# An MLP's second product by Strassen's scheme, over pairs of token tiles, in a four-layer decoder trunk on eight cores

## The chip, the cores and the metric

The kernel runs on the 8 NeuronCores of one Trainium2 chip. Each core takes one of the 8 sequences of the batch and works alone on it, with all weights. The time is device time in microseconds of the slowest core. A measurement of this kernel is the median of some runs; the three runs of the kernel before lie between 3194.84 and 3195.68 us.

## What is computed

The input is (8, 2048, 1024) in float32. Four layers follow each other, then a last RMSNorm. Each layer adds a token mixer and then an MLP to the residual x:

```python
for i in range(4):
    h = rmsnorm(x, norm_mix[i])
    x = x + mixer[i % 3](h)          # A: chunked gMLP, B: pooling, C: Conformer convolution
    h = rmsnorm(x, norm_mlp[i])
    x = x + jnp.square(jax.nn.relu(h @ m_w1[i])) @ m_w2[i]   # 1024 -> 4096 -> 1024
out = rmsnorm(x, norm_final)
```

So the layers' mixers are A, B, C, A. An MLP is two products, each of 2048 x 1024 x 4096 per core.

## The kernel before

**Layout.** x stays in SBUF in float32 for the whole kernel, transposed (`xT`: 128 partitions, 8 chunks `kc` of the width, 2048 tokens), as four token tiles `tt` of 512. Products are in bf16: a matmul takes a 128x128 block of weights as the stationary operand and 512 tokens as the moving one, and accumulates in one of 8 PSUM banks (128 x 512 float32). Weights come by DMAs that GpSimd issues, into a ring of five slots of 8 KB per partition (`take_slot`, `load_w`); the DMA turns float32 into bf16.

**Order.** The kernel is first written down as a list of operations (`sc.op`) with an estimated cost each; `Sched.schedule` (L219) then makes, in advance, an order for each engine: among the operations that can start earliest it takes the one written first. It also gives out the banks, and holds two back for older operations (`RESERVE`). The order on each engine is fixed from then on; semaphores keep the dependencies. Every operation is issued from a helper, so all rows of the profile show its line, L161, and are told apart by the tiles that they write and read.

**MLP** (`mlp`, L678). The inner width of 4096 is cut into 8 blocks `fb` of 512. `W1(fb, tt)` makes 4 groups of 8 matmuls into a bank each; VectorE applies the ReLU and the norm's factor `rst` (one `scalar_tensor_tensor` from the bank to a float32 buffer `rl`), ScalarE squares it into the bf16 tile `aT`. `W2(fbs, tt)` makes 8 groups, one for each output chunk `dc`, of 4 matmuls per `fb`; after each group VectorE adds the bank to x (`add_to_x`, L665). W1 of the next pair (fb, tt) is written ahead of W2 of the current one. The outer loop goes over `fb`, the inner over the four tiles, so each weight block is loaded once. In layers 0, 2 and 3 the last two blocks share their bank in W2. Ahead of the first use of a tile, `prep` scales x by the norm's gain into h (half the chunks on ScalarE, half on VectorE) and sums the squares (squares on ScalarE, sums on GpSimd or VectorE, one matmul to sum over partitions, then logarithm and exponential on ScalarE).

**Passes.** When a tile has had its last block, `after_tile` of the next mixer starts that mixer's norm of the tile: A for tile 0, B for tiles 0 and 1 and the factors of the others, C scaled copies `c_h` of all four tiles and their sums of squares, with a spill of part of x to HBM. Mixer C's first product needs all four tiles, since it takes every sixteenth token. Mixer A's gate tables `a_S` (`setup`, L788: 24 small VectorE operations, two loads by SyncE, a mask on GpSimd) are made within the MLP ahead of it, in layer 0 within its own body (L1016). In the last layer the last tile's W2 is cut into 256, 128 and 128 columns, so that the final norm and the store can start early. The folded weights of mixer B are made at the head of its body (L1098), before its first product S1(0).

Of the kernel before, what the change touches and what calls it, by code (L numbers as in the profile page):

```python
# [15 lines left out]
KC = 8  # L16
# [65 lines left out]

class Res:
# [41 lines left out]
    def split(self, n):  # L125

        l = []
        for _ in range(n):
            x = Res()
            x.w, x.r = set(self.w), set(self.r)  # L130
            l.append(x)
        self.subs += l
        return l
# [30 lines left out]
def MM(out, lhsT, rhs, start, stop):  # L164
    return I("matmul", out, lhsT=lhsT, rhs=rhs, start=start, stop=stop)

# [253 lines left out]
def c_dve(n=512, mode=1):  # L420
    return 0.09 + n / (960.0 * mode)
# [10 lines left out]
HT_OFF = 54 * KB  # L432
# [3 lines left out]
def build_program(S, layers, final):  # L436
# [32 lines left out]
    if layers:  # L469
        din("m_w1", (4, 8, 128, 4096))  # L470
        din("m_w2", (4, 8, 128, 4096))
# [36 lines left out]
    epst, (eps_res,) = pers("epst", (128, 1), F32)  # L508
    mhalf, (mh_res,) = pers("mhalf", (128, 4), F32)
# [64 lines left out]
    sc.op("dve", I("memset", epst[:], EPS), wr=[eps_res])  # L574
    sc.op("pool", I("memset", mhalf[:], -0.5), wr=[mh_res])
# [8 lines left out]
    def sum_squares(tt, acc, acc_r, eng="pool", after=(), cs=slice(0, 512)):  # L584

        n = cs.stop - cs.start
        for kc in range(KC):
            sq, sq_r = (sacc, sacc_r) if kc == 0 else next_sq()[::2]
            sc.op("act", I("activation", out=sq[:, cs], in_=xs(kc, tt)[:, cs], func=AF.Square),
                  rd=[xr(kc, tt, cs)], wr=[sq_r], cost=c_act(n), after=after, tag="sq")  # L590
            if kc:
                last = kc == KC - 1
                sc.op(eng, I("tensor_tensor", out=acc[:, cs] if last else sacc[:, cs], in0=sacc[:, cs], in1=sq[:, cs], op=ALU.add),
                      rd=[sq_r, sacc_r] if last else [sq_r], wr=[acc_r if last else sacc_r],
# [63 lines left out]
    def rmsnorm(tt, gcol, hT, hr, mode="pool", rs=None, after=()):  # L658
        rs, rs_r = rs or rms(tt, None, mode, after=after)
        for kc in range(KC):  # L660
            sc.op("dve", I("scalar_tensor_tensor", out=hT[:, kc, :], in0=xs(kc, tt),
                           scalar=pv[:, gcol + kc:gcol + kc + 1], in1=rs, op0=ALU.mult, op1=ALU.mult),
                  rd=[xr(kc, tt), rs_r, pv_res], wr=[hr[kc]], cost=c_dve(), port=True, tag="hT")

# [4 lines left out]
    def mix_h(i):  # L669
# [4 lines left out]
    PLACES = {0: ((0, 8, 16, 30), (24, 26, 28, 38), (70, 74, 40), (78, 80, 82)),  # L674
              1: ((54, 0, 8, 32), (50, 40, 42, 44), (46, 66), (52, 62, 64)),
              2: ((0, 8, 16, 24), (46, 48, 50, 52), (32, 36, 62), (40, 42, 44))}

    def mlp(l, after_tile, mode, last, setup):  # L678
        gcol = PCOLS[f"norm_mlp{l}"]
        p_h, p_rs, p_a, p_rl = PLACES[l % 3]  # L680
        hT, aT, rl, rst, w = [], [], [], [], {}

        def prep(tt):
            hT.append(zone(f"mh{tt}", (128, KC, 512), BF16, p_h[tt] * KB, KC))
            h, hr = hT[tt]
            rst.append(zone(f"mrs{tt}", (128, 512), F32, p_rs[tt] * KB))
            for kc in range(KC):
                scale_x(kc, tt, gcol, h[:, kc, :], [hr[kc]], "dve" if kc % 2 else "act")
            rms(tt, (rst[tt][0][:], rst[tt][1][0]), mode[tt])

        def load(fb):
            w[fb] = (load_w("m_w1", l, fb, (8, 512)),
                     load_w("m_w2", l, fb, (4, 1024)))

        def W1(fb, tt):
            if fb == 0:
                prep(tt)
# [25 lines left out]
        def W2(fbs, tt, parts=((0, 512),)):  # L723

            for p0, p1 in parts:
# [10 lines left out]
                while ends:  # L736
                    ends.pop()()
# [888 lines left out]
```

How the kernel before makes its waits and increments, by code:

```python
            def body(e):  # L382
                table = None
                if eng == "act":
                    table = "lnexp"
                    e.preload_act_table_set(TABLES[table])
                for lst, o in plan[eng]:
                    for k, v in lst:
                        e.wait_ge(sems[k], v)
                    if o.table is not None and o.table != table:
                        table = o.table
                        e.preload_act_table_set(TABLES[table])
                    for f in o.fns[:-1]:
                        f(e)
                    o.fns[-1](e).then_inc(sems[o.pos], 1 if o.dma is None else 16)
                if eng == "sp":
                    for k in self.dma_keys:
                        if per.get(k) and known["sp"].get("D_" + k, 0) < 16 * len(per[k]):
                            e.wait_ge(sems["D_" + k], 16 * len(per[k]))
                    for f in self.ENGS:
                        if f != "sp" and known["sp"].get("E_" + f, 0) < cnt["E_" + f]:
                            e.wait_ge(sems["E_" + f], cnt["E_" + f])
```

## Time and profile before

| | |
|---|---|
| median of three runs | 3195.46 us |
| profiled execution, slowest core (5), span | 3193.6 us |
| spans of the eight cores | 3186.4 to 3193.6 us |
| TensorE busy, matmuls | 3163.5 us (99%), 16042 |
| VectorE, ScalarE, GpSimd busy | 1988.0, 976.4, 510.4 us |
| mean granted TensorE clock | 0.997 to 0.998 |

The profile records one execution of its own; its time is known as the spans of its cores, and the runs of the first row are others of the same program. Busy times are sums over the instructions of an engine, shares are of the span. A matmul's duration (379 ns for 512 columns) overlaps the next one's; the interval between starts is what counts. "Idle before, releaser" is how long the engine stood still ahead of a group and what ended that.

### The profile page before, as it was taken

What the parts mean: (1) busy time and instruction counts of PE and PEld (TensorE: products, weight loads), DVE (VectorE), ACT (ScalarE), POOL (GpSimd) and SP (SyncE); (2) the same over time, 40 slices, a digit from 0 to 9 for tenths busy, and PEclk for the clock granted to TensorE, in tenths of its full rate; (3) what the DMA queues carried; (4) which work ended last, traced back from release to release, by engine and by line L of the source; (5) the groups of instructions that cost most, each with busy time, mean ns of one, the idle gap of its engine ahead of it and who ended that gap; (6) DMA issues with size and microseconds to landing.
All of it is one profiled execution on the core that took longest, in us unless ns stands there. A gap on an engine that the chain in (4) does not pass through costs nothing.

```text
span 3193.6 us, 45998 instructions; the slowest of 8 cores (3186.4 to 3193.6 us)
## 1 busy us (share of the span) xinstructions
PE 3163.5 (99%) x16042; PEld 1518.9 (48%) x16042; DVE 1988.0 (62%) x3152; ACT 976.4 (31%) x1621; POOL 510.4 (16%) x527
## 2 busy tenths in 40 slices
PE   8999999999999999999999999999999999999999
PEld 4444444444444444444576444444444444444444
DVE  8945665665556965665558666654755757466556
ACT  4312433211134431112634511121322333311124
POOL 1111322100022010000551300010212141200011
PEclk9999999999999999999999999999999999999999
DMA  9599898122216412221422422214898987522202
GB/s 169 105 158 169 158 163 136 27 40 40 40 25 109 72 27 40 40 39 20 109 46 81 67 53 41 40 27 68 138 162 131 155 147 136 92 40 38 42 14 106
DMA packets 82398, 264.44 MB, mean 83 GB/s; under 512 B 4992, under 2 KB 8192, under 8 KB 82176
## 3 DMA queue, kind: packets, MB, share of 16 engines
q0 software_dynamic: 64992, 231.49, 43.3%
q1 hardware_dynamic: 17184, 30.02, 3.0%
q8 instruction: 135, 2.21, 0.3%
q14 instruction: 87, 0.71, 0.1%
HBM read 479.34 MB, written 13.63 MB: 154 GB/s over the span
## 4 chain that ended last, share of the span: by engine, by line
PE 97%; DMA 1%; ACT 1%; DVE 1%; issue 0%; POOL 0%; SPq 0%; DVEq 0%; ACTq 0%; POOLq 0%
PE bank L161 97%; DMA xT<-x 1%; DMA ring_46<-b_w_out 0%; DMA ring_45<-a_w_in 0%; DVE sacc L161 0%; ACT ring_47 L161 0%; DVE xT L161 0%; SPq L161 0%; DVE c_y L161 0%; ACT c_h_138 L161 0%; ACT L392 0%; ACT hraw_75 L161 0%; DVE c_z_166 L161 0%; POOL sacc L161 0%; ACT xT L161 0%
## 5 line engine op out<-in xcount | busy, mean ns | idle before, releaser
L161 DVE TENSOR_TENSOR xT<-bank,xT 128x512 f32<-128x512 f32 (+2 forms) x1040 | 707.6, 683 | 449.8 <-PE bank L161 439.4
L161 ACT ACTIVATE a_uT<-bank,pv 128x512 bf16<-128x512 f32 x96 | 65.6, 686 | 145.1 <-PE bank L161 141.8
L161 ACT ACTIVATE a_uTv_192<-bank,pv 128x512 bf16<-128x512 f32 x96 | 65.9, 686 | 96.4 <-PE bank L161 96.3
L161 ACT ACTIVATE a_vv_188<-bank 128x512 bf16<-128x512 f32 x96 | 56.9, 597 | 102.4 <-DVE bank L161 102.3
L161 DVE SCALAR_TENSOR_TENSOR bank<-bank,pv,a_Sv_182 128x512 f32<-128x512 f32 x96 | 71.5, 757 | 25.7 <-PE bank L161 25.6
L161 DVE SCALAR_TENSOR_TENSOR bank<-bank,pv,a_S 128x512 f32<-128x512 f32 x96 | 71.2, 755 | 25.2 <-PE bank L161 25.0
L161 POOL TENSOR_TENSOR sacc<-sacc,sq_58 128x512 f32<-128x512 f32 (+1 forms) x52 | 65.0, 1250 | 108.8 <-ACT sq_58 L161 58.4
L161 DVE BATCH_NORM_STATS2 a_stv_190<-a_vv_188 128x6 f32<-128x512 bf16 x96 | 65.7, 687 | 26.6 <-ACT a_vv_188 L161 26.6
L161 POOL TENSOR_TENSOR sacc<-sacc,sq_56 128x512 f32<-128x512 f32 (+1 forms) x52 | 65.1, 1253 | 102.2 <-ACT sq_56 L161 93.4
L161 DVE TENSOR_TENSOR bank<-bank,a_bvbv_189 128x512 f32<-128x512 f32 x96 | 66.1, 688 | 17.7 <-PE bank L161 17.7
L161 DVE TENSOR_TENSOR a_uTv_192<-bank,a_uTv_192 128x512 bf16<-128x512 f32 x96 | 65.1, 689 | 11.7 <-DVE bank L161 9.5
L161 POOL TENSOR_TENSOR sacc<-sacc,sq_60 128x512 f32<-128x512 f32 (+1 forms) x52 | 65.7, 1264 | 36.3 <-ACT sq_60 L161 26.7
L161 DVE TENSOR_TENSOR a_uT<-bank,a_uT 128x512 bf16<-128x512 f32 x96 | 64.9, 687 | 9.6 <-DVE bank L161 8.7
L161 ACT ACTIVATE sq_58<-xT 128x512 f32<-128x512 f32 (+1 forms) x84 | 52.0, 619 | 53.7 <-POOL sacc L161 26.8
L161 ACT ACTIVATE sq_56<-xT 128x512 f32<-128x512 f32 (+1 forms) x84 | 51.8, 616 | 46.3 <-DVE xT L161 24.9
L161 ACT ACTIVATE sq_60<-xT 128x512 f32<-128x512 f32 (+1 forms) x84 | 52.0, 619 | 42.0 <-DVE xT L161 23.1
L392 ACT ACT_TABLE_LOAD x19 | 24.4, 1283 | 130.1 <-DVE bank L161 111.3
L161 ACT ACTIVATE a_v<-bank 128x512 bf16<-128x512 f32 x72 | 42.4, 596 | 68.5 <-DVE bank L161 68.3
L161 DVE BATCH_NORM_STATS2 a_st<-a_v 128x6 f32<-128x512 bf16 x72 | 48.9, 687 | 16.9 <-ACT a_v L161 16.8
L161 POOL DMA_DIRECT2D ring_45<-m_w x14 | 10.0, 716 | 274.6 <-PE bank L161 274.6
L161 POOL DMA_DIRECT2D ring_48<-m_w x13 | 9.4, 719 | 250.7 <-PE bank L161 231.6
L161 POOL DMA_DIRECT2D ring_47<-m_w x12 | 8.6, 717 | 253.2 <-PE bank L161 253.2
(924 smaller groups left out, 6680.9 us busy)
## 6 DMA issues: line engine op xcount, KB each, us to landing
ring_46<-a_w_in POOLq DMA_DIRECT2D x19, 1024.0 KB, 12.0
ring_45<-a_w_in POOLq DMA_DIRECT2D x19, 1024.0 KB, 11.9
ring_44<-a_w_in POOLq DMA_DIRECT2D x18, 1024.0 KB, 13.4
ring_48<-a_w_in POOLq DMA_DIRECT2D x17, 1024.0 KB, 12.8
ring_47<-a_w_in POOLq DMA_DIRECT2D x15, 1024.0 KB, 13.4
ring_45<-m_w POOLq DMA_DIRECT2D x14, 1024.0 KB, 8.7
ring_48<-m_w POOLq DMA_DIRECT2D x13, 1024.0 KB, 8.9
ring_44<-m_w POOLq DMA_DIRECT2D x13, 1024.0 KB, 8.3
```

Of the source, the lines that this page charges most:

```text
L161: return lambda e: getattr(e, _method)(*[_r(a) for a in args], **{k: _r(v) for k, v in kwargs.items()})
L392: e.preload_act_table_set(TABLES[table])
```

## The change

The second product of the MLP is computed by Strassen's scheme in Winograd's form. The outer loop takes pairs of token tiles (`p`), the inner one four blocks `b` of 1024 of the inner width. For a pair and a block, the activations are A11, A12 (first tile, both halves of the block) and A21, A22 (second tile), the weights W11 to W22 (first digit: half of the block, second digit: output chunk d or d + 4). `G1` makes the activations with the first product; its ReLU runs on ScalarE within the bank where h already carries the norm's factor, and on VectorE for tiles 0 and 1 of layer 2. `sums` makes four sums of activations, `load2` loads four weight tiles of one d and makes four sums of them, all in bf16 on VectorE. `G2` makes seven products of four matmuls each into four banks; two banks are accumulated into after they have been read, and each read of a bank is an add into x (eight per d). The very last block of the last layer stays plain (`plain_block`, with the cuts of before). Since p is the outer loop, `m_w1` and `m_w2` are loaded once per pair, hence twice; a load of `m_w2` is half as large as before. h of tiles 0 and 1 is made during the mixer before (`early`), that of tiles 2 and 3 in steps between the G2 of the first pair; the next mixer's norms of tiles 0 and 1 in steps during the second pair. Mixer A's `setup` is always in its body, mixer B's comes after S1(0), and the places of the buffers are new. The diff, cut to its core:

```diff
+def MORE(out, lhsT, rhs, start, stop):
+    return I("matmul", out, lhsT=lhsT, rhs=rhs, start=start, stop=stop, skip_group_check=True)
...
-    return 0.09 + n / (960.0 * mode)
+    return 0.155 + n / (960.0 * mode)
...
+    H_BLK = 4
+    POOL_OFF = 32 * KB
+    POOL_N = 53
+    def c_fast(n=512):
+        return 0.09 + n / 1900.0
...
+        def prep(tt, mode):
+            if raw_first and tt < 2:
+                h[tt] = mix_h4(tt)
+                hT, hr = h[tt]
+                for kc in range(KC):
+                    scale_x(kc, tt, gcol, hT[:, kc, :], [hr[kc]], "dve" if kc % 2 else "act")
+                rst[tt] = rms(tt, None, mode)
+                yield
+            else:
+                if tt == 2:
+                    rsx_.append(zone("m_rsx", (128, 512), F32, POOL_OFF + POOL_N * KB))
+                rs = rms(tt, (rsx_[0][0][:], rsx_[0][1][0]) if tt >= 2 else None, mode)
+                yield
+                h[tt] = mix_hall(tt) if l % 3 == 1 else mix_h4(tt)
+                yield from rmsnorm_steps(tt, gcol, *h[tt], rs=rs)
...
+        def G1(p, b, i):
+            if i % 2 == 0:
+                w1[(p, b, i // 2)] = load_w("m_w1", l, b * 2 + i // 2, (32, 128))
+            w, wr_ = w1[(p, b, i // 2)]
+            for n, t in ((0, 1), (1, 1), (0, 0), (1, 0)):
+                tt = 2 * p + t
+                hT, hr = h[tt]
                 bk = Bank()
+                for k0, k1 in ((0, 6), (6, 7), (7, 8)) if raw_first and first[0] else ((0, KC),):
+                    sc.op("pe", [MM(bk.v(), w[:, (i % 2 * 2 + n) * KC + kc, :], hT[:, kc, :], kc == 0, kc == KC - 1)
+                                 for kc in range(k0, k1)], rd=[wr_] + hr[k0:k1], wr=[bk], cost=c_pe(k1 - k0), tag="W1")
+                if tt in rst:
+                    sc.op("dve", I("scalar_tensor_tensor", out=bk.v(), in0=bk.v(), scalar=0.0, in1=rst[tt][0],
+                                   op0=ALU.max, op1=ALU.mult), rd=[rst[tt][1]], wr=[bk], cost=c_dve(), tag="relu")
+                else:
+                    sc.op("act", I("activation", out=bk.v(), in_=bk.v(), func=AF.Relu), wr=[bk], cost=c_act(), tag="relu")
+                a, ar = A[(p, b, i, "A%d%d" % (t + 1, n + 1))] = tile()
+                sc.op("act", I("activation", out=a[:], in_=bk.v(), func=AF.Square), rd=[bk], wr=[ar], cost=c_act(), tag="sqr")
+            first[0] = False
+        def comb(out, o_r, x, x_r, y, y_r, op):
+            sc.op("dve", I("tensor_tensor", out=out, in0=x, in1=y, op=op), rd=[r for r in (x_r, y_r) if r is not o_r], wr=[o_r],
+                  cost=c_fast(), port=True, tag="comb")
+        def sums(p, b, i):
+            def get(k):
+                return A[(p, b, i, k)]
+            def put(k, x, y, op, to=None):
+                t, r = A[(p, b, i, k)] = to or tile()
+                comb(t[:], r, get(x)[0][:], get(x)[1], get(y)[0][:], get(y)[1], op)
+            put("S1", "A21", "A22", ALU.subtract)
+            put("m2", "A11", "S1", ALU.subtract)
+            put("m3", "A21", "A11", ALU.subtract, get("A21"))
+            put("n4", "A12", "m2", ALU.subtract)
+        def load2(b, d, plain=False):
+            t, r, key = take_slot()
+            last_load[0] = sc.op("pool", I("dma_start", out=t[:, 0:2048], in_=dram["m_w2"][l, b * 4 + d], max_dma_last_dim=8192), wr=[r],
+                                 cost=0.95, dma=key, nbytes=512 * 2048, tag="load")
+            w_ops.append(last_load[0])
+            v = {k: t[:, j * 512:(j + 1) * 512] for j, k in enumerate(("W11", "W12", "W21", "W22", "T1", "n2", "T4"))}
+            vr = dict(zip(v, r.split(7)))
+            if not plain:
+                comb(v["T1"], vr["T1"], v["W12"], vr["W12"], v["W11"], vr["W11"], ALU.subtract)
+                comb(v["W12"], vr["W12"], v["W22"], vr["W22"], v["W12"], vr["W12"], ALU.add)
+                comb(v["n2"], vr["n2"], v["W22"], vr["W22"], v["T1"], vr["T1"], ALU.add)
+                comb(v["T4"], vr["T4"], v["W21"], vr["W21"], v["n2"], vr["n2"], ALU.subtract)
+            return {k: v[k].rearrange("p (i c) -> p i c", i=4) for k in v}, vr
+        def G2(p, b, d):
+            w, wr_ = load2(b, d)
+            x11, x12, x21, x22 = ((d, 2 * p), (d + 4, 2 * p), (d, 2 * p + 1), (d + 4, 2 * p + 1))
+            a, f, e, g = Bank(), Bank(), Bank(), Bank()
+            def prod(bk, ak, wk, start, outs):
+                mm = MM if start else MORE
+                ts = [A[(p, b, i, ak)] for i in range(H_BLK)]
+                sc.op("pe", [mm(bk.v(), w[wk][:, i, :], ts[i][0][:], start and i == 0, i == H_BLK - 1) for i in range(H_BLK)],
+                      rd=[wr_[wk]] + [r for _, r in ts], wr=[bk], cost=c_pe(4), tag="W2")
+                for dc, tt in outs:
+                    add_to_x(dc, tt, bk)
+            prod(a, "A11", "W11", True, [x11])
+            prod(f, "A12", "W21", True, [x11])
+            prod(e, "m3", "W12", True, [x22])
+            prod(a, "m2", "n2", False, [x21])
+            prod(g, "n4", "W22", True, [x12])
+            prod(e, "A22", "T4", False, [x21])
+            prod(a, "S1", "T1", False, [x12, x22])
...
+        early = [prep(tt, "pool") for tt in range(2)]
+        yield early
+        for e in early:
+            run_all(e)
+        pipe = [(p, b) for p in range(2) for b in range(4)]
+        for i in range(H_BLK):
+            G1(0, 0, i)
+            sums(0, 0, i)
+        for j, (p, b) in enumerate(pipe):
+            more = j + 1 < len(pipe)
+            if (p, b) == (0, 0):
+                work.extend(prep(tt, "pool") for tt in (2, 3))
+            if (p, b) == (1, 0):
+                work.extend(gen_store(tt) if last else nxt.after_steps(tt) for tt in (0, 1))
+            if (p, b) == (1, 3) and not last:
+                work.extend(iter(nxt.late_steps(tt)) for tt in (0, 1))
+            while (p, b) == (0, 3) and work:
+                step()
+            for i in range(H_BLK):
+                plain = last and not more
+                if more and i < H_BLK - 1:
+                    G1(*pipe[j + 1], i)
+                if not plain:
+                    G2(p, b, i)
+                elif i == 0:
+                    while work:
+                        step()
+                    plain_block(p, b)
+                if more:
+                    if i == H_BLK - 1:
+                        G1(*pipe[j + 1], i)
+                    if not (last and j + 2 == len(pipe)):
+                        sums(*pipe[j + 1], i)
+                step()
+        while work:
+            step()
+        if not last and nxt:
+            for tt in (2, 3):
+                run_all(nxt.after_steps(tt))
+                run_all(nxt.late_steps(tt))
...
+    hall = nc.alloc_sbuf_tensor_at("hall", [128, KC, S], BF16, offset=Z0)
+    def mix_hall(tt):
+        return hall[:, :, tt * 512:(tt + 1) * 512], [Res(Z0 + kc * 2 * S + tt * 1024, Z0 + kc * 2 * S + tt * 1024 + 1024) for kc in range(KC)]
...
-                    if first:
-                        self.setup(UOFF, after=third[:1])
+                    self.setup(UOFF, after=third[:1])
...
+        def after_steps(self, tt):
+            h, hr = mix_hall(tt)
+            for j, kc in enumerate(KORDER):
+                self.hr[kc][tt] = hr[kc]
+                scale_x(kc, tt, self.gcol, h[:, kc, :], [hr[kc]], "act")
+                if tt < 2 and j % 2:
+                    yield
+            sp_dma(f"spill{tt}", x_spill[tt], xT[:, 3:8, tt * 512:(tt + 1) * 512], rd=[xr(kc, tt) for kc in range(3, 8)],
+                   nbytes=128 * 5 * 2048)
+            yield
+        def late_steps(self, tt):
             if not self.started:
                 self.start()
-            h = self.h
-            xg = [scale_x(kc, tt, self.gcol, h[kc][:, tt * 512:(tt + 1) * 512], [self.hr[kc][tt]], "act") for kc in range(KC)]
-            if tt < NT - 1:
-                sum_squares(tt, self.acc[:, tt * 512:(tt + 1) * 512], self.acc_r[tt])
-            else:
-                sum_squares(tt, self.acc[:, tt * 512:(tt + 1) * 512], self.acc_r[tt], "dve", after=[xg[5]])
-            sp_dma(f"spill{tt}", x_spill[tt], xT[:, 3:8, tt * 512:(tt + 1) * 512], rd=[xr(kc, tt) for kc in range(3, 8)],
-                   nbytes=128 * 5 * 2048)
-        def body(self, first):
+            sum_squares(tt, self.acc[:, tt * 512:(tt + 1) * 512], self.acc_r[tt], "dve" if tt == NT - 1 else "pool", order=KORDER,
+                        run=(rsb[0][0], rsb[0][1][0]) if tt == NT - 1 else None)
...
-        shared["m_w1"] = tiles(f("m_w1"), 8, 512)
-        shared["m_w2"] = tiles(f("m_w2"), 4, 1024)
+        w1 = f("m_w1").reshape(-1, KC, 128, 4, 2, 2, 2, 128).transpose(0, 3, 5, 2, 6, 4, 1, 7)
+        shared["m_w1"] = w1.reshape(-1, 8, 128, 4096)
+        w2 = f("m_w2").reshape(-1, 4, 2, 4, 128, 2, 4, 128).transpose(0, 1, 6, 4, 2, 5, 3, 7)
+        shared["m_w2"] = w2.reshape(-1, 16, 128, 2048)
```

## Rows read from the trace of the kernel before

**Rows 1.** Cores: span and mean granted TensorE clock (core 5 is on the second die).
```profile
core 0: 3186.4 us, clock 0.998
...
core 5: 3193.6 us, clock 0.997
```
**Rows 2.** The page's busy line: us, share of the span, instructions of each engine.
```profile
PE 3163.5 (99%) x16042; PEld 1518.9 (48%) x16042; DVE 1988.0 (62%) x3152; ACT 976.4 (31%) x1621; POOL 510.4 (16%) x527
```
**Rows 3.** Chain of waits: shares of the span by engine.
```profile
PE 97%; DMA 1%; ACT 1%; DVE 1%; issue 0%; POOL 0%; SPq 0%; DVEq 0%; ACTq 0%; POOLq 0%
```
**Rows 4.** Windows: us, busy us (instructions) by engine, granted clock, DMA share, GB/s.
```profile
80.00:160.00 80.00, 80.00 (x443) 39.16 (x441) 74.82 (x139) 26.29 (x41) 10.84 (x18) 1.00 0.60 106
...
544.00:986.00 442.00, 441.99 (x2048) 200.24 (x2047) 258.98 (x378) 119.44 (x196) 57.42 (x56) 1.00 0.23 41
...
592.70:648.00 55.30, 55.30 (x258) 25.09 (x257) 33.25 (x49) 10.07 (x16) 1.43 (x2) 1.00 0.21 39
```
**Rows 5.** Timeline of TensorE, two W2 calls: start us, us, operation.
```profile
1540.35 7.07 PE L161 MATMUL bank<-aT0v_130,ring_45 128*128 128x512 bf16 x32
1547.25 7.07 PE L161 MATMUL bank<-aT1v_133,ring_45 128*128 128x512 bf16 x32
```
**Rows 6.** Waits of TensorE from 60 to 3160 us: sum us, times, longest.
```profile
PE bank L161 <- DMA ring_46<-b_w_out: 2.2, 1, 2.2
...
PE bank L161 <- ACT c_h_139 L161: 1.3, 1, 1.3
```
**Rows 7.** Groups of VectorE by form: busy us, mean ns, idle before.
```profile
L161 DVE TENSOR_TENSOR xT<-bank,xT 128x512 f32<-128x512 f32 x1016 | 700.8, 691 | 447.3 <-PE bank L161 436.9 <-issue 0.3
...
L161 DVE BATCH_NORM_STATS2 a_stv_190<-a_vv_188 128x6 f32<-128x512 bf16 x96 | 65.7, 687 | 26.6 <-ACT a_vv_188 L161 26.6
...
L161 DVE TENSOR_TENSOR sacc<-sacc,sq_60 128x512 f32<-128x512 f32 x20 | 13.7, 687 | 5.3 <-ACT sacc L161 3.3 <-ACT sq_60 L161 1.1 <-DVE sacc L161 0.9
...
L161 DVE SCALAR_TENSOR_TENSOR rl_89<-bank,mrs_92 128x512 f32<-128x512 f32 x11 | 7.6, 692 | 10.5 <-PE bank L161 10.5
...
L161 DVE SCALAR_TENSOR_TENSOR a_S<-bank,pv,a_bs 128x128 f32<-128x128 f32 x24 | 6.4, 343 | 0.0
...
L161 DVE SCALAR_TENSOR_TENSOR hT_73<-xT,pv,rs_64 128x512 bf16<-128x512 f32 x8 | 5.5, 745 | 1.6 <-ACT rs_64 L161 1.6
...
L161 DVE TENSOR_TENSOR xT<-bank,xT 128x128 f32<-128x128 f32 x16 | 3.9, 284 | 1.6 <-PE bank L161 1.6
...
L161 DVE TENSOR_SCALAR hT_74<-xT,pv 128x512 bf16<-128x512 f32 x8 | 3.6, 491 | 6.5 <-DMA xT<-x 6.5
...
L161 DVE TENSOR_TENSOR xT<-bank,xT 128x256 f32<-128x256 f32 x8 | 3.0, 417 | 0.9 <-PE bank L161 0.9
...
L161 DVE TENSOR_TENSOR c_T_156<-ring_47,c_mask 128x1536 bf16<-128x1536 bf16 x1 | 0.9, 948 | 0.0
```
**Rows 8.** Groups of ScalarE by form.
```profile
L161 ACT ACTIVATE a_vv_188<-bank 128x512 bf16<-128x512 f32 x96 | 56.9, 597 | 102.4 <-DVE bank L161 102.3
...
L161 ACT ACTIVATE mh_85<-xT,pv 128x512 bf16<-128x512 f32 x4 | 2.7, 709 | 0.0
```
**Rows 9.** Timeline of VectorE within a W2 call.
```profile
2962.71 0.69 DVE L161 TENSOR_TENSOR xT<-bank,xT 128x512 f32<-128x512 f32 x1 [0.17 <-PE bank L161]
2963.57 0.69 DVE L161 TENSOR_TENSOR xT<-bank,xT 128x512 f32<-128x512 f32 x1 [0.17 <-PE bank L161]
```
**Rows 10.** Tile mh3v_180 (ns min/median/max, first and last start), and GpSimd's adds.
```profile
L161 DVE TENSOR_SCALAR mh3v_180<-xT,pv x4: 474/981/1490, 1768.5 to 1781.5; 128x512 bf16<-128x512 f32 x4
...
L161 POOL TENSOR_TENSOR sacc<-sacc,sq_60 128x512 f32<-128x512 f32 x50 | 63.5, 1270 | 35.9 <-ACT sq_60 L161 26.7 <-POOL sacc L161 4.5 <-ACT sacc L161 3.2
```
**Rows 11.** DMA: the whole span, one queue in 592.7 to 648, an issue row.
```profile
DMA packets 82398, 264.44 MB, mean 83 GB/s; under 512 B 4992, under 2 KB 8192, under 8 KB 82176
...
q0 software_dynamic: 542, 2.09, 20.7%
...
ring_44<-m_w POOLq DMA_DIRECT2D x13, 1024.0 KB, 8.3
```

More of the change, by code:

```diff
@@ L431 @@
 KB = 1024
-HT_OFF = 54 * KB
+HT_OFF = 0
 SM_OFF = 70 * KB
@@ L582, in next_sq, with sum_squares @@
         return sqb[sqn[0] % NSQ]
[L584 removed]
+    def sum_squares(tt, acc, acc_r, eng="pool", after=(), cs=slice(0, 512), order=range(KC), run=None):
         n = cs.stop - cs.start
[L587 to L588 removed]
+        run, run_r = run or (sacc, sacc_r)
+        for k, kc in enumerate(order):
+            sq, sq_r = (run, run_r) if k == 0 else next_sq()[::2]
             sc.op("act", I("activation", out=sq[:, cs], in_=xs(kc, tt)[:, cs], func=AF.Square),
                   rd=[xr(kc, tt, cs)], wr=[sq_r], cost=c_act(n), after=after, tag="sq")
[L591 to L594, printed above, removed]
+            if k:
+                last = k == KC - 1
+                sc.op(eng, I("tensor_tensor", out=acc[:, cs] if last else run[:, cs], in0=run[:, cs], in1=sq[:, cs], op=ALU.add),
+                      rd=[sq_r, run_r] if last else [sq_r], wr=[acc_r if last else run_r],
                       cost=c_pool(n) if eng == "pool" else c_dve(n), port=True, tag="sqadd")
@@ L663, in rmsnorm, with run_all @@
                   rd=[xr(kc, tt), rs_r, pv_res], wr=[hr[kc]], cost=c_dve(), port=True, tag="hT")
+            if k % 2:
+                yield
+    def run_all(steps):
+        for _ in steps or ():
+            pass
+    def rmsnorm(*args, **kwargs):
+        run_all(rmsnorm_steps(*args, **kwargs))
     def add_to_x(dc, tt, bk, cs=slice(0, 512)):
@@ new lines, in plain_block, with step, gen_store @@
+            ends.pop()()
+        ends = []
+        work = []
+        def step(n=1):
+            for _ in range(n):
+                if work and next(work[0], work) is work:
+                    work.pop(0)
+        def gen_store(tt):
+            end = nxt(tt)
+            yield
+            end()
+        early = [prep(tt, "pool") for tt in range(2)]
[6 more added lines that the diff above has]
+            sums(0, 0, i)
@@ L1030, in body @@
                     self.norm(tt + 1, after=[late_u[0]])
+                else:
+                    for e in early:
+                        run_all(e)
                 WO(tt, mid)
@@ L1182, in body @@
                         self.norm(tt + 2)
+                if tt in (1, 2):
+                    next(early[tt - 1])
+                elif tt == 3:
+                    for e in early:
+                        run_all(e)
                 S2(tt)
```

233 lines of the change are left out of this document (97 added, 136 removed).

## The prediction

> **What bounds the kernel now.** I first looked at the cores: all eight lie within 7.2 us, and the granted clock is 0.998 in core 0 and 0.997 in core 5, that is the 2.4 GHz level on either die [rows 1]. The profile is of core 5, span 3193.6 us. The median of the runs is 3195.46 us, so about 1.9 us lie around the span; I make the sum against the span and add them. Next the page's busy line [rows 2]: TensorE 99%, VectorE 62%, ScalarE 31%. The chain of waits says the same, 97% of it matmuls [rows 3]. The windows show that the MLP stages are the purest case [rows 4]: in 544 to 986 (layer 0's MLP) 2048 matmuls fill 442.0 us without a gap, 0.2158 us each; the timeline gives 32 matmuls from 1540.35 to 1547.25, 6.90 us, 0.2156 each [rows 5]. The list of what TensorE waited for has no entry from an MLP stage except the end of the last one; between 60 and 3160 us it holds nine entries that sum to 9.8 us, none over 2.2, of which some 2.6 us are the pass from layer 1's MLP to mixer C and 2.2 us a late `b_w_out` load [rows 6]. So time here is the number of matmuls, as long as the other engines keep up.
>
> **What the change takes away.** A block is one pair of token tiles by 1024 of the inner width. The second product of a block is now 2 tiles x 8 output chunks x 8 = 128 matmuls; with seven products for eight it is 4 values of d x 7 products x 4 = 112. There are 4 layers x 2 pairs x 4 blocks = 32 blocks, of which the very last stays plain: 31 x 16 = 496 matmuls fewer. They sit in stages where TensorE never rests, so each is worth its full interval: 496 x 0.216 = **107.1 us**. The first product keeps its count, and so do the norms. All matmuls stay 128x128 by 512 in bf16.
>
> **VectorE.** (a) Per block 16 sums of activations and 16 of weights, all 128x512 in bf16 from SBUF to SBUF, 992 in all. No row has this shape. From above: an fp32 sum of 512 takes 687 to 691 ns; from below: the bf16 product of 1536 elements takes 948 ns [rows 7]. The adds of 512, 256 and 128 columns (691, 417, 284) give a fixed 150 ns or so [rows 7]; (948 - 150)/1536 = 0.52 ns per element, so 150 + 266 = 416 ns. I take 0.416 us, since the 948 row has the same operation, type and memory, and keep 0.69 as the upper end, 0.32 (948/3) as the lower. (b) The adds into x: a block needs 4 x 8 = 32. Before, a layer needed 224 (six blocks of 512 one by one, two merged), layer 1 had 256. Now 256 each, and 232 wide ones in the last layer for 216: 80 more of 0.691, 55 us. (c) The ReLU leaves VectorE except for tiles 0 and 1 of layer 2: 512 - 64 = 448 fewer of 0.691, minus 310 us. (d) Preparing h: eight 0.745 ops for fourteen tiles, against four cheaper scalings, about +50 us. Sum: 413 + 55 - 310 + 50 = +208 us, 1988 to 2196, or 71% of the new span. In an ordinary block: 32 x 0.691 + 32 x 0.416 = 35.4 us in 240 x 0.216 = 51.8 us of matmuls, 68%; now it is 33.3 in 55.3, 60% [rows 4]. In the first half of layer 2 each step (32 + 28 matmuls, 12.96 us) also has 4 ReLUs and a share of the preparation of tiles 2 and 3: 5.53 + 3.33 + 2.76 + 0.75 = 12.4 us, 95%. The window 80 to 160 has VectorE at 74.8 of 80 us, 94%, with TensorE at 80.0 [rows 4]: such a load alone stops nothing. I put 3 us on these 16 steps for what the order written out in advance gets wrong, with 0 and 30 as ends.
>
> **ScalarE and the banks.** The 448 ReLUs go there, PSUM to PSUM. The nearest row is PSUM to SBUF, 597 ns, and a scaled copy within SBUF takes 709 [rows 8]; I take 0.6, with 0.71 as the upper end (21.0 us a block, still 40%). With squares of about 0.6 too: 19.2 of 51.8 us, 37%, and 976 + 448 x 0.6 - 14 x 4 x 0.71 = 1205 us in the whole. That hides beside TensorE. But a bank is now held for ReLU and square, some 1.3 us with the semaphores, instead of 0.7. A group of eight matmuls takes 1.73 us, so the first product holds two to three banks, and the second product four. Seven of eight: it fits.
>
> **The new wait.** Bank a gets three products and bank e two; each next one must wait until the adds have read the last. Two other products (8 matmuls, 1.73 us) lie between. From the timeline of adds [rows 9]: one starts every 0.86 us, takes 0.69 and leaves 0.17 idle. A matmul is 0.379 long at an interval of 0.216, so a result is there some 0.2 us after its product's turn; add 0.69 and the semaphore, and the bank is free 0.95 to 1.0 us after the product, 0.7 before it is wanted. One sum (0.42) pushed in between doesn't use that up, two would. Behind a waiting product stand all later matmuls of TensorE's queue, the next G1 as well; the planner orders them by its own costs (0.36 for a sum, where I have 0.416). Its planned order is kept, so I charge 3 us for 124 G2 calls, with ends 0 and 0.3 us each (37 us).
>
> **GpSimd.** What the profile shows of VectorE beside it: a scaling of 512 elements has 491 ns for tile 0's `hT_74`, but 474, 981 and 1490 for `mh3v_180`, while GpSimd's adds of 1270 ns run [rows 7, 10]. The Trainium skill (SBUF — State Buffer, "Who interferes with whom") says that a VectorE instruction with two SBUF inputs and a GpSimd instruction that reads SBUF block each other for a whole instruction. By it every bf16 sum beside such an add could wait up to 1.27 us; the trace agrees in kind by the 981. In the rows alone: a layer's MLP has 28 such adds, at most 36 us of VectorE in some 415, which lifts it from about 72% to 81%, below the 94% seen with a full TensorE. I charge nothing in the ordinary blocks; in layer 2 it is within the end of 30 above.
>
> **Loads.** Both weights are now read once per pair, so the 64 loads of 1024 KB become twice as many bytes, 67.1 MB more, 331.5 in all [rows 11]. In one step of 55.3 us before, 2.09 MB took 20.7% of the sixteen engines, 11.4 us [rows 11]; a block now moves 4.19 MB, 23 us in 51.8. Each load has a slot more than a step (13 us) before its use, and lands in 8.3 to 8.9 us. Nothing waits. GpSimd issues at about 0.7 us, six per block, 4 us in 52.
>
> **Passes between stages.** Tiles 2 and 3 now finish together. The last block of layers 0 to 2 has four G2 in a row without G1: 8 adds are 5.5 us in 6.05, 91%, plus weight sums that can be made ahead. TensorE can go on with the next mixer, whose h of tiles 0 and 1 is made earlier (A and B), or with chunks in the order 0, 4, 1, 5, 2, 6 (C). For C two tiles' last scalings and squares end on ScalarE, 8 x 0.66 = 5.3 us, then 0.7 us adds, against some 8.7 us of projections; I keep its 2.6 us of waits and add 1. For B the fold follows S1(0); six loads want five slots and one of b_w_in waits for the fold: the 2.2 us stay. Layer 3's mixer A makes its 24 S tiles (24 x 0.343 = 8.2 us) in the first V stage, where VectorE has 24 bias adds and 24 statistics of 0.69 [rows 7], 33 of 41.5 us, anyway; U groups free their banks by ScalarE and can run ahead: 1 us. From C to layer 2's MLP both tiles' norms go over GpSimd, 14 adds of 1.27; tile 1's factor comes some 14 us after the last x, but six banks are enough for its groups until then: 1 us. The end is as before. Together 3 us, ends -2 and 15.
>
> **Sum.** 3193.6 - 107.1 + 3 + 3 + 3 = 3095.5 us of span, +1.9: **3097 us**, 3.1% less. If all three losses are nothing and 2 us are won: 3086.
>
> **Rivals.**
> (1) *VectorE becomes the bound in places*: the bf16 sums take 0.69 instead of 0.416. For it: the only 512-wide SBUF sums in the trace do. Against: the 948. A usual step is then 5.5 + 5.5 = 11.1 of 12.96; in layer 2's first half 5.53 + 5.53 + 2.76 + 0.75 = 14.6, over by 1.6, x 16 = 26 us; the bare G2 add some 5. 3097 + 31 = 3128.
> (2) *Banks a and e come back late*, by 0.3 us per G2: 124 x 0.3 = 37 in place of 3, 3131. For it: adds every 0.86 us leave only 0.17 for anything else. Against: 0.7 us of slack.
> (3) *The passes cost the 15 us or more* (a cold ring, the S tiles, both tiles' norms): 3109 to 3115.
> (4) *Slower than before*, in one mechanism: the order written out ahead puts sums in front of the adds, so that each of the three reuses in a G2 waits. It decides at 107.1/124 = 0.86 us per G2, 0.29 per reuse, that is 1.0 us of delay with the slack of 0.7, two to three sums or ReLUs before each add. With 0.4 per reuse: 149 us, 3195 - 107 + 149 = 3237. Against it: VectorE has a third of its time free in 28 of 32 blocks.
> (5) *The change doesn't save matmuls*: excluded by the count in the code; that the accumulation after a stop costs TensorE an extra drain would be 3 reuses x 124 x 0.16 (0.379 - 0.216) = 61 us at worst, 3158. No row shows it.
>
> **How the numbers follow.** The forecast (3086 to 3106) 0.58; (3) 0.13; (1) and (2) 0.08 and 0.09; (5) 0.05; (4) 0.06 and 0.01 for a result near no change. A range of 3084 to 3136 holds all but (4), (5) and the far parts of (1) and (2): 0.84. Two tenths of a per cent, 6.4 us, is about what a measurement of this kernel tells from no change. Faster by more: 0.93; within: 0.01; slower: 0.06.
>
> **What would show it.** Right: some 15546 matmuls, clock still 0.99 or more; a middle block in 52 us; bf16 sums near 0.42 and ReLUs near 0.6; VectorE near 2200 us, ScalarE near 1205; about 331 MB; waits of TensorE on `xT` under 5 us in total. (1) would show as sums of 0.69 and waits in layer 2's MLP; (2) and (4) as TensorE waiting for VectorE in each G2, some 0.3 or over 0.86 us; (3) as waits within 30 us of a pass; (5) as an interval over 0.22 with no wait named. The prediction is wrong if blocks take over 54 us.

## The result, and the profile after

| | median us | |
|---|---|---|
| before | 3195.15 (3194.11 to 3195.68) | |
| changed | 3118.46 (3117.02 to 3120.32) | ratio 0.976, 95% interval 0.9746 to 0.9773 |
| forecast | 3097, range 3084 to 3136 | |

Faster by 2.4%, within the range and 21 us above the number. All medians and ratios here leave out executions in which one half of the chip ran at a lower granted clock, and one that was kept but stands 20 us or more above its fellows is named.

The page's busy line and DMA lines of the changed kernel answer to [rows 2, 11].

```profile
span 3118.8 us, 46054 instructions; the slowest of 8 cores (3109.1 to 3118.8 us)
...
PE 3049.2 (98%) x15253; PEld 1473.4 (47%) x15546; DVE 2130.7 (68%) x3804; ACT 1184.3 (38%) x2013; POOL 616.0 (20%) x683
...
DMA packets 100841, 331.60 MB, mean 106 GB/s; under 512 B 7040, under 2 KB 10240, under 8 KB 100608
```

The weight loads (`PEld`, whose records are complete) are 15546, as many as forecast: 496 fewer. The moved bytes are the forecast 331.6 MB. TensorE is still the bound, at 98%.

The windows of two blocks of layer 0's MLP and of the first two of layer 2's answer to [rows 4] (instructions in brackets, then clock, DMA share, GB/s):

```profile
546.00:597.80 51.80, 51.54 (x237) 23.53 (x240) 26.82 (x56) 30.89 (x52) 5.66 (x7) 1.00 0.47 85
597.80:649.60 51.80, 51.54 (x237) 23.48 (x240) 33.04 (x65) 18.87 (x32) 3.57 (x6) 1.00 0.46 82
1745.00:1796.80 51.80, 49.63 (x224) 22.18 (x228) 39.66 (x66) 29.76 (x53) 30.78 (x26) 1.00 0.46 80
1796.80:1848.60 51.80, 51.59 (x238) 23.48 (x241) 48.64 (x94) 9.55 (x16) 3.63 (x6) 1.00 0.48 85
```

A block of 240 loads takes the 51.8 us that 240 x 0.216 gives. The last row is worth a look: VectorE is at 48.6 of 51.8 us, 94%, and TensorE doesn't notice. The row above it, with VectorE at only 77% but GpSimd at 30.8 us, is the one that loses, 12 loads' worth. VectorE's load alone doesn't decide.

TensorE's waits in the same execution from 60 to 3090 us (sum us, times, longest), where [rows 6] had nothing over 2.2:

```profile
PE bank L164 <- DVE xT L164: 5.7, 5, 2.4
...
PE bank L164 <- DVE b_pl L164: 5.3, 1, 5.3
...
PE bank L164 <- DMA ring<-b_w_in: 3.6, 1, 3.6
...
PE bank L164 <- ACT hall L164: 2.1, 1, 2.1
...
PE bank L164 <- DVE mh1v L164: 1.7, 1, 1.7
```

**A table by stage.** A list of waits has no stages and leaves out what a wait costs afterwards. So I took from the traces, on every core, the starts of successive weight loads and summed by how much each interval exceeds 0.216 us (only excesses above 0.03), cutting the stages at the same count of matmuls in all kernels. This holds waits, and matmuls at the lower level of the clock. It is one execution of each kernel; a stage that an edit doesn't touch still differs by up to 1.3 us between two kernels. Mean of eight cores:

| stage | before | after | more |
|---|---|---|---|
| start, mixer A of layer 0 | 14.5 | 16.2 | 1.7 |
| MLP 0 | 2.0 | 3.8 | 1.8 |
| mixer B | 2.3 | 14.9 | **12.6** |
| MLP 1 | 0.7 | 1.4 | 0.7 |
| mixer C, pass to MLP 2 | 13.1 | 17.9 | **4.8** |
| MLP 2 | 1.4 | 6.7 | **5.3** |
| mixer A of layer 3 | 1.1 | 2.3 | 1.3 |
| MLP 3 and the end | 4.2 | 9.6 | 5.4 |
| sum | 39.3 | 73.0 | 33.7 |

Of the 107.1 us that the matmuls are worth, some 31 to 34 didn't arrive (from the first to the last weight load, the mean of the cores fell by 76.6). The forecast had allowed 9.

### The profile page after: what moved, and what is told of

The parts are those of the page before. It is cut to its first block, busy times and chain, and to the rows that moved or that the text cites. A ratio compares the mean times of both kernels' runs of the same rounds, so it can differ in the third digit from the quotient of the medians.

```text
span 3118.8 us, 46054 instructions; the slowest of 8 cores (3109.1 to 3118.8 us)
## 1 busy us (share of the span) xinstructions
PE 3049.2 (98%) x15253; PEld 1473.4 (47%) x15546; DVE 2130.7 (68%) x3804; ACT 1184.3 (38%) x2013; POOL 616.0 (20%) x683
## 4 chain that ended last, share of the span: by engine, by line
PE 93%; DMA 2%; DVE 2%; issue 2%; ACT 1%; another core or an unknown queue 0%; POOL 0%; SPq 0%; DVEq 0%; ACTq 0%; POOLq 0%
PE bank L164 93%; DMA ring<-m_w 1%; DMA xT<-x 1%; DVE xT L164 0%; DMA ring<-b_w_in 0%; DVE m_tv L164 0%; DMA ring<-a_w_in 0%; ACT ring L164 0%; DVE ring L164 0%; DVE b_pl L164 0%; ACT sq L164 0%; ACT m_tv L164 0%; DVE hall L164 0%; ACT rs L164 0%
## 5 line engine op out<-in xcount | busy, mean ns | idle before, releaser
L164 PE MATMUL bank<-m_tv,ring 128*128 128x512 bf16 (+2 forms) x3653 | 792.8, 373 | 12.3 <-DVE xT L164 8.2
L164 PEld LDWEIGHTS bank<-m_tv,ring 128*128 128x128 bf16 x3724 | 359.3, 98 | 430.9 <-issue 19.6
L164 ACT ACTIVATE bank<-bank 128x512 f32<-128x512 f32 x448 | 260.8, 582 | 658.2 <-PE bank L164 640.3
L164 DVE TENSOR_TENSOR m_tv<-m_tv,m_tv 128x512 bf16<-128x512 bf16 x494 | 211.3, 448 | 339.6 <-ACT m_tv L164 338.3
L164 ACT ACTIVATE m_tv<-bank 128x512 bf16<-128x512 f32 x511 | 304.5, 597 | 163.7 <-DVE bank L164 122.8
L164 POOL TENSOR_TENSOR sacc<-sacc,sq 128x512 f32<-128x512 f32 (+1 forms) x180 | 232.2, 1290 | 164.4 <-ACT sq L164 100.8
L164 DVE TENSOR_TENSOR ring<-ring 128x512 bf16<-128x512 bf16 x496 | 211.0, 444 | 47.9 <-DMA ring<-m_w 37.5
L164 PE MATMUL bank<-hall,ring 128*128 128x512 bf16 x1003 | 223.7, 379 | 1.1
L164 PE MATMUL bank<-mh,ring 128*128 128x512 bf16 x1002 | 223.0, 379 | 1.1
L164 PE MATMUL bank<-a_uTv,ring 128*128 128x512 bf16 x752 | 165.9, 379 | 0.9
```

The costliest lines, as they stand in the source:

```text
L164: return lambda e: getattr(e, _method)(*[_r(a) for a in args], **{k: _r(v) for k, v in kwargs.items()})
```

## The experiments

Times are set against the changed kernel's 3118.5. Each kernel starts from the changed one.

**1. Eight products in the same structure.**
```diff
-            w, wr_ = load2(b, d)              # and sums() returns at once
+            w, wr_ = load2(b, d, True)
-            prod(a, "A11", "W11", True, [x11])    # ... seven of these
+            pair(a, 1, 1, x11)                    # 8 matmuls, one add, four of these
```


> Eight block products in place of seven, with no bf16 sums and four adds into x per d instead of eight; all else (pairs of tiles outside, loads twice, norms in steps, the passes) stays. 31 blocks x 16 = 496 matmuls more, 107.1 us at 0.216. Theory T1 (the seven products cost nothing but their matmuls; what the forecast missed lies in the passes between stages, mixer B above all): the changed kernel's 3118.5 + 107, less up to 5 for a lighter VectorE, 3220 to 3227 us. Rival T2 (the sums, adds and bank reuse of the seven products hold TensorE up in the blocks): the eight products win part of the 107 back, at or under 3205 us.

Measured: 3213.0 (spans of its cores 3205.1 to 3211.4) and 3239.5. In the second, two cores have 3237 and 3238 at a clock of 0.987, and the other six 3203.2 to 3210.5, as in the first. So I read the first; by the mean of both (3226.2) the seven products would be worth 107.7 us. The cores bear the choice out: in halves of the chip at a clock of 0.99 or more, over all executions, the mean span of a core is 3208.4 us (20 cores) against 3112.5 (32 cores) in the changed kernel, 95.9 apart, where the first gives 94.5. That lies between the two theories: some 95 us of the 107.1 come from the seven products and some 12 are lost to them; and the structure alone, with as many matmuls as before, is 18 us slower than before. In its stages mixer B's excess is 14.9, as in the changed kernel: B's loss has nothing to do with Strassen's scheme. The MLPs have 1.3, 0.8, 2.5 and 1.3.

**2. No bf16 sums.**
```diff
-            put("S1", "A21", "A22", ALU.subtract)     # and three more, and four of weights
+            A[(p, b, i, "S1")] = get("A22")           # plain tiles under the names of the sums
```


> The seven products stay, but all 992 bf16 sums are left out: the products take the plain tiles instead, so the values of the MLP differ from the reference's. T1: the sums (0.44 us each, 422 us of VectorE in all) are hidden, and only the gaps in layer 2's MLP and some in the passes shrink: 3108 to 3118 us. T2: VectorE's load is what costs, 3100 us or less.

Measured: 3108.3 (3107.1 to 3109.7), 10 us less. At the edge of the first theory. So nearly all that the seven products cost beyond their matmuls is their sums, 422 us of VectorE, of which 97% is hidden. By stage (mean of cores 0 to 3 of both kernels): C and the pass to MLP 2 3.6 us less, the MLPs 0.9, 0.2, 1.3 and, with the end, 1.9.

**3. Each sum twice.**
```diff
+            for _ in range(2):
                 sc.op("dve", I("tensor_tensor", out=out, in0=x, in1=y, op=op), ...)
```


> Each of the 992 bf16 sums is made twice (those in place thus give other values than the reference's). Per step of 12.96 us of matmuls VectorE then has 8 x 0.69 + 16 x 0.444 = 12.6 us, and in layer 2's first half 12.6 + 2.8 + 0.75 = 16.2. T1 (VectorE decides only where its load passes TensorE's): 16 steps x 3.2 = 51 us in layer 2, and 0 to 40 us for a load of 97% elsewhere, 3170 to 3210 us. T2 (VectorE binds already): most of the added 440 us shows, over 3400 us.

Measured: 3153.7 (3149.9 to 3155.4, and one run at 3178.4), 35 us more for 440 us of added VectorE work. The place was right, the size too large: of the added time 25 us are in MLP 2, where I had 51. Some 9 are in the last block of layer 1's MLP, where four G2 stand without first products, and 3 in mixer B; the other blocks of the other MLPs have almost none, though a step there is 97% full by the count. VectorE decides where its load passes TensorE's, and hardly earlier.

The count itself is too high. VectorE's instructions overlap: one that needn't wait starts before the last has ended, after a bf16 sum 0.335 us from its start (its row says 0.42), after an add into x 0.60 us (0.69). Two rows of the changed kernel's timeline, the second starting 0.33 us behind the first (start us, us):

```profile
609.12 0.41 DVE L164 TENSOR_TENSOR m_tv<-m_tv,m_tv 128x512 bf16<-128x512 bf16 x1
609.45 1.29 DVE L164 TENSOR_TENSOR xT<-bank,xT 128x512 f32<-128x512 f32 x2
```

So a block of layer 0 with doubled sums has VectorE busy for 45.6 to 46.6 of 51.8 us, 88 to 90%, with TensorE full.

**4. No other product between two into a bank.**
```diff
+            prod(a, "A11", "W11", True, [x11])
+            prod(a, "m2", "n2", False, [x21])
+            prod(a, "S1", "T1", False, [x12, x22])
+            prod(e, ...), prod(e, ...), prod(f, ...), prod(g, ...)
```


> The seven products in another order: the three into bank a one after the other, then the two into bank e, then f and g, so that no other product of the same G2 stands between a product and the next one into its bank. An add's delay is about 0.95 us after the product; with three reuses in 124 G2 calls 353 us if nothing fills them. T1 (the reuse is covered by other matmuls, and the written-out order finds first-product groups to put between): 3120 to 3160 us, the loss mostly where no first product is left to put between (the last blocks). T2 (reuse already costs with two products between): well over 3200 us.

Measured: 3148.5 (3147.3 to 3150.3), +30, within the first range: 6.6, 7.3, 3.6 and 5.5 us in the MLPs and 4.2 in mixer C's stage. But the place isn't the expected one. The loss doesn't sit mostly in the last blocks; TensorE loses 1 to 3 us in nearly every block that has first products as well, outside the first half of layer 2. The largest of the waits by name:

```profile
PE bank L164 <- DVE xT L164: 11.9, 14, 2.5
```

So the two products between are worth something, 30 us of the 353 that the adds' delays come to; what covers the rest no run shows. With the spacing of the change the reuse costs next to nothing: on core 0 from 600 to 780 us the 833 intervals between 834 weight loads average 0.2159 and only one stands out (0.449).

**5. Eight pooled tiles in mixer B.**
```diff
-            win = [zone(...) for i in range(3)]      # 4 KB each
-            pool_ = [zone(...) for i in range(6)]    # 2 KB each
+            win = [zone(...) for i in range(2)]
+            pool_ = [zone(...) for i in range(8)]
```


> Mixer B only: eight pooled tiles in place of six, and two window buffers in place of three, so that the last tile's pooling need not wait until S2(2) has read its buffers. Theory B1 (the 5.3 us wait ahead of S2(3) is this buffer wait: before the change W1 of the next MLP stood there, now its h isn't made yet): the wait goes, 5 to 8 us less than the changed kernel's 3118.5, 3110 to 3114. Rival B2 (VectorE is simply full there, with the early norms of the MLP's tiles and GpSimd in its way): 0 to 2 us less.

Measured: 3111.7 (3110.8 to 3114.8), 6.8 less, as the first theory had it; mixer B is 6.9 us shorter, no other stage changed by over 1.3. Core 0's waits in B before and after the edit:

```profile
PE bank L164 <- DVE b_pl L164: 5.3, 1, 5.3
PE bank L164 <- ACT b_wf L164: 2.4, 2, 2.1
```
```profile
PE bank L164 <- ACT b_ca L164: 2.8, 1, 2.8
PE bank L164 <- ACT b_wf L164: 0.6, 2, 0.3
```

The wait for `b_pl` is gone; a shorter one took its place. The sequence in the changed kernel is plain in VectorE's timeline (start us, us): S2(2) reads the last of two buffers at 1078.3, only then can the last two poolings be written, and each takes 1.7 us where it takes 1.22 elsewhere.

```profile
1073.69 3.35 DVE L164 SCALAR_TENSOR_TENSOR hall<-xT,pv,rs 128x512 bf16<-128x512 f32 x2
...
1080.11 3.41 DVE L164 SCALAR_TENSOR_TENSOR b_pl<-b_w,b_px 128x1024 bf16<-128x1024 f32 x2
1083.44 8.37 DVE L164 SCALAR_TENSOR_TENSOR hall<-xT,pv,rs 128x512 bf16<-128x512 f32 x11
1091.73 0.74 DVE L164 SCALAR_TENSOR_TENSOR xT<-bank,b_cb,xT 128x512 f32<-128x512 f32 x1
```

TensorE had nothing to put there, since 11 of the 16 parts of the next MLP's h come after it. Before the change the last tile's poolings ran from 1098.3 to 1105.8, and nobody waited: the first W1 of the next MLP ran from 1097.6 to 1106.4.

**6. b_wgs off the ring.**
```diff
-            wgs, wgs_r, _ = take_slot()
+            wgs, wgs_r = zone("b_wgs", (128, KC, 256), BF16, self.wgs_off, KC)
```


> Mixer B only: the scaled group weights b_wgs lie in a place of their own (that of two pooled tiles not yet in use) instead of a ring slot, so five loads want five slots. Theory R1 (the wait for b_w_in at the second S1 comes from the sixth claim on the ring): 2.4 to 3.6 us of wait go, 3113 to 3116 us. Rival R2 (the loads are late because of the bytes ahead of them in the queue): no change, 3117 to 3120.

Measured: 3116.5 (3115.8 to 3116.5, and one run at 3144.5), B 4.1 us shorter by its stage. The two ranges (3113 to 3116, 3117 to 3120) miss it by the half microsecond between them; the stage speaks for the sixth claim. Core 2's wait for `b_w_in` fell from 2.4 to 1.5 us and that for `b_pl` from 5.3 to 4.6. That is 1.6 us of waits, and the rest goes with the clock: in the changed kernel core 2 was at the lower level for 6.8 us from 983.1 and for 6.8 from 1075.3, with the edit for 3.4 from 1076.1 alone.

**7. Mixer B's early sums of squares on VectorE.**
```diff
-        early = [prep(tt, "pool") for tt in range(2)]
+        early = [prep(tt, "dve" if l % 3 == 1 else "pool") for tt in range(2)]
```


> Layer 1 only: the sums of squares of tiles 0 and 1, made within mixer B, go to VectorE (14 x 0.69 us) instead of GpSimd (14 x 1.27). Theory G1 (GpSimd's adds lock VectorE's operations with two SBUF inputs: in the changed kernel 0.419 becomes 0.997 us for a bf16 sum, 0.744 becomes 1.28 or more for an h operation, when they overlap): what VectorE does more, 9.7 us, is about what it no longer loses; the wait of S2(3) falls from 5.3 to about 3 us, 3114 to 3119 us. Rival G2 (no lock, VectorE just has too much to do in B): the wait grows by up to the 9.7 us, 3122 to 3128.

Measured: 3117.8 (3116.5 to 3119.3). 9.7 us more work for VectorE in the place where it is fullest, and B took the same time to 0.02 us; the wait for `b_pl` went from 5.3 to 4.8. What VectorE got it no longer lost: the mean of its 16 `hall` operations there fell from 0.976 to 0.759 us. So the conflict is seen in the durations, but the edit won no time.

**8. All sums of squares for the MLPs' norms on VectorE.** As 7 for all layers, and for tiles 2 and 3; `b_wgs` and the pooled tiles as in the changed kernel.
```diff
-                work.extend(prep(tt, "pool") for tt in (2, 3))
+                work.extend(prep(tt, "dve") for tt in (2, 3))
```

> All sums of squares for the MLPs' own norms on VectorE (4 layers x 28 x 0.69 = 77 us more), none on GpSimd. Theory G1 (the lock is what makes sums long): bf16 sums fall from a mean of 0.446 to about 0.42 us, and with a third of VectorE free the time stays, 3110 to 3122 us, better in layers 0 and 3, worse in layer 2's first half (95% full). Rival G2 (load decides, the lock is nothing): 5 to 20 us more, 3124 to 3138, mostly in layer 2.

Measured: 3112.4 and 3139.9, ratio to before 0.978 (0.972 to 0.984). The total decides nothing: the interval holds the changed kernel, and the lower one lies in the first range, the mean of both (3126.1) in the second. By the mean span of the cores at a clock of 0.99 or more (24 cores, 3109.0) the edit wins 3.5 us. The stages are clearer (mean of cores 0 to 3 of both kernels): MLP 2's excess falls from 6.2 to 1.7, the pass to it from 2.4 to 0.4, together 5 us of elapsed time, and that in the layer which I had counted as fullest. Elsewhere MLP 3 with the end is 3.7 us longer and MLP 0 1.8, so on these four cores nothing is left of it. Core 0's waits from 1690 to 2150 us, changed kernel and this one:

```profile
PE bank L164 <- DVE mh1v L164: 1.6, 1, 1.6
PE bank L164 <- DVE xT L164: 1.3, 2, 0.9
PE bank L164 <- ACT rs L164: 0.9, 1, 0.9
```
```profile
PE bank L164 <- ACT ring L164: 1.5, 1, 1.5
```

The wait for `mh1v` is the conflict at work. Three scalings of h in a row, which take 0.49 us each when no such add runs, took 5.2 us beside GpSimd's adds in the changed kernel (core 4), and TensorE waited 1.7 us for the first of the last two:

```profile
1740.25 1.97 DVE L164 TENSOR_SCALAR mh0v<-xT,pv 128x512 bf16<-128x512 f32 x1
1742.14 3.35 DVE L164 TENSOR_SCALAR mh1v<-xT,pv 128x512 bf16<-128x512 f32 x2
```

It hangs on a few tenths of a microsecond: in experiment 7, which leaves layer 2 alone, the first of the three took 0.60 us (core 0), and the wait was gone. The wait for `rs` is another matter: the edit also makes the sums ahead of the norm's factor faster, 0.69 us each for 1.27, and no run takes the two apart.

**9. Sums of weights written later.**
```diff
-                o.end = dma_free + self.DMA_LAT
+                o.end = dma_free + self.DMA_LAT + (4.0 if o.nbytes == 512 * 2048 else 0.0)
```


> Only the planner's idea of the loads of m_w2 (and of the one other load of 512 KB) is changed: they count as landing 4 us later, so that sums of weights come later in VectorE's written-out order. Theory L1 (sums of weights at the head of VectorE's queue, waiting for a load, 37.5 us in 54 waits in the changed kernel, hold the adds behind them and by them TensorE, 2.4 us at 790.9 us): VectorE's waits for m_w fall to under 15 us, and 2 to 6 us go from the MLPs of layers 0, 2 and 3, 3112 to 3117 us. Rival L2 (that idle time is VectorE's spare third and costs nothing): 3117 to 3120 us.

Measured: 3119.5 (3118.8 to 3120.7), no gain. The total is the rival's. In the stages both theories are half right: MLP 0 and 3 are 2.1 and 2.4 us shorter, MLP 2 0.9 and the pass to it 1.3, and VectorE's waits for `m_w`, 37.5 us before, are gone from the list; but the end became 5.7 us longer and B and C 1.4 and 1.6, where the last blocks' weights now come too late in the order.

**10. Edits 5, 6 and 8 (layers 1 and 2 only) together.**
```diff
-        early = [prep(tt, "pool") for tt in range(2)]
+        early = [prep(tt, "dve" if l in (1, 2) else "pool") for tt in range(2)]
```

> What the runs before point to, together: eight pooled tiles and b_wgs off the ring in mixer B, and the sums of squares of the MLPs of layers 1 and 2 on VectorE. From the stages of the single runs: B 7.3 + 4.1 - some overlap = 10 us, layer 2 and the pass to it 7 us. Theory (the three are independent, and the forecast's missing time lies there): 3118.5 - 17 = 3102 us, 3098 to 3106. Rival (a gain in one place comes back as another wait, such as VectorE in mixer B, where these sums also lie): 3107 to 3112.

Measured: 3105.6 (3101.3 to 3106.4, and one run at 3146.6), at the upper edge of the first range; ratio to before 0.974 (0.966 to 0.983), so the total alone doesn't tell it from the changed kernel. B is 10.5 us shorter, where the single edits add up to 11.0; layer 2 and its pass 5.2 of 7.

**11. The same, with 9's edit in blocks 0 to 2 of layers 0, 2 and 3.**
```diff
+    tag="late" if b < 3 and l != 1 else "load"       # in load2; 4 us later for "late"
```


> The three edits of mixer B and layers 1 and 2 together, as in the combination before, and besides the loads of m_w2 counted as landing 4 us later, but only in blocks 0 to 2 of layers 0, 2 and 3, not at their ends. Theory L1 (by stages: 2 us each in the MLPs of layers 0 and 3, up to 1 in layer 2; the 5.7 us that the same edit cost at the very end, and the 1.4 and 1.6 in mixers B and C, came from the last blocks' loads): 3 to 6 us less than the combination's 3105, 3099 to 3102. Rival (moving the sums always costs at the next pass what it wins in the blocks, as in the run with the edit alone): 3103 to 3107.

Measured: 3099.3 (3098.0 to 3100.7), ratio to before **0.9695 (0.9681 to 0.9708)**: 19 us less than the changed kernel and the fastest of all. The MLPs of layers 0 and 3 give their 2.0 and 2.4, B 10.4, and the end keeps its time.

## Right and wrong, step by step

The stated range holds the result, but the core of the forecast, 3086 to 3106 with a chance of 0.58, does not: the three losses were put at 9 us and came to some 31, and what lies above was in the range only through the upper ends of the terms. Two signs were missed too: TensorE waited 5.7 us for `xT` between 60 and 3090 us and 8.2 in all, where I had under 5, and VectorE was busy for 2131 us, not near 2200.

**Right: the price of the matmuls.** 496 fewer by the count, 0.216 each in blocks of 51.8 us. **Right: the bf16 sum.** 0.416 us was read off the 948 ns row [rows 7]; the tile's rows (ns min/median/max) show 0.420 where nothing is in the way, and ScalarE's tiles the 0.6 that was taken:

```profile
L164 ACT ACTIVATE m_tv<-bank x511: 573/597/610, 550.9 to 3076.3; 128x512 bf16<-128x512 f32 x171
L164 DVE TENSOR_TENSOR m_tv<-m_tv,m_tv x494: 408/420/1775, 554.6 to 3025.6; 128x512 bf16<-128x512 bf16 x165
```

**Right: the bank reuse** costs under the 3 us given (4), and rivals (1), (2), (4) and (5) didn't come. **Right within its ends, less so in kind: 3 us on layer 2's full steps.** MLP 2 lost 5.3. Experiment 3 shows that VectorE becomes the bound there first, but in the changed kernel the load of 94% alone cost nothing in the window above, and experiment 8 took most of the loss away while it loaded VectorE more.

**Wrong: the price of GpSimd beside VectorE.** I charged nothing in the ordinary blocks and left it within the upper end of the 3 us in layer 2, and the passes had no term for it. This is the 1775 ns in the row above. In the changed kernel's trace a bf16 sum takes 0.419 us at the median where no add of GpSimd overlaps it (947 sums) and 0.997 where one does (45); an h operation 0.744 and 1.28. Operations that read one operand from PSUM take 0.691 either way. That is the rule of the Trainium skill which I had weighed (SBUF — State Buffer, "Who interferes with whom"), and the trace now shows it for two inputs in SBUF. I had set its price by VectorE's total, which indeed doesn't matter, where it works by delay: three scalings held up in a row at the pass into layer 2. Those have one tensor as input and not two, like the 981 ns row; seven of them beside such an add took 1.537 us at the median instead of 0.489. Experiment 7 shows the conflict in the durations, experiment 8 what its edit is worth, some 5 us in layer 2 and the pass to it; how much of that is the conflict and how much the faster sums isn't shown. I had also overlooked that the change moves 28 sums of squares (three tiles of layer 1, one of layer 2) from VectorE to GpSimd. It brought the conflict to the two fullest places. It is also a small part (18 us) of why VectorE came to 2131 us and not 2196. The larger part is the overlap of experiment 3: the sum of the durations of its instructions rose by 239 us, more than the forecast 208, but the busy time by 143, since the overlap of successive instructions rose from 94 to 190 us.

**Wrong: "Together 3 us" for the passes.** The term measured about 20, mixer B 12.6 of it; rival (3) with its 15 us named the kind. I looked for what is late after the last MLP block and not for what the new structure takes away from the end of a mixer. Two tiles of h must be whole before G1 can begin, and they lie where mixer B's buffers are until its last pooling; so nothing covers that pooling any more (experiment 5, 7 us). In the ring I had seen the six claims on five slots and written "the 2.2 us stay": `b_wgs` cost 4, time at the lower clock included (experiment 6).

**Wrong: "Nothing waits" for the loads.** TensorE doesn't wait for a weight load in the blocks, but a sum of weights at the head of VectorE's queue does, with adds behind it: the slot is there in time, the bytes mostly (54 waits, the longest 4.1 us). Experiments 9 and 11 put 2 us each on layers 0 and 3; in experiment 9 alone the ends of the stages gave it all back.

What stays open: 2.8 us at the end (a 2.4 to 2.7 us wait for x in the plain last block), 2.9 in mixer C (the 2.1 us wait for `hall` at the pass to it is gone in experiment 2, so it comes from the sums), and 1.7 at the start, where the change touches only places of buffers.

## What to carry to other kernels

Seven products for eight paid most of the 107 us that it is worth (95 by experiment 1), since the engine that does the sums had a third of its time free; most of what was lost lay outside of the loop that was changed. When a loop's order is turned round, ask at each pass what filled the gaps there before, and whether its inputs are still ready. And price two engines that hold each other up by where they meet, not by the sum of their times; and a full VectorE by the distance of its starts, not by the durations of its rows.

## What the runs showed of the hardware

- A VectorE operation with both tensors in SBUF took 0.997 instead of 0.419 us (bf16 sum) or 1.28, at most 1.786, instead of 0.744 (h) while a GpSimd add of 1.27 us ran; with one operand in PSUM nothing changed (0.691 in 98 adds into x beside one, 0.691 in 966 without). A scaling with a single tensor in SBUF, float32 to bf16, was held up too (1.537 for 0.489, seven of them); the bf16 sums' medians beside an add differ between the cores, 0.73 to 1.16.
- VectorE's instructions overlap: when nothing held it, the instruction behind a bf16 sum of 0.42 us started 0.335 us after the sum's start, and behind an add of 0.69 us 0.60 after the add's.
- In the middle of core 4 TensorE waited 1.9, 2.1, 2.4, 3.6 and 5.3 us, and its granted clock was at its lower level (1.2 of 2.4 GHz) for 3.4 us at each of the first four and for 6.8 at the last, 20.5 us in all, against two stretches of 3.4 us in core 5 before (waits of 2.2 and 1.9). Part of each stretch lies in the wait itself, so a wait of 5.3 us cost more than it shows in the list of waits.
- An accumulation that goes on in a bank after VectorE has read it, with the group formally ended, ran at the usual 0.216 us per matmul.
